# A mixture-of-experts stage on one core: the last expert's fourth up slot comes in as two transfers, and the combination stands ahead of every fourth up slot

## The reference

```python
# w_gu: (32, 1024, 2048), w_dn: (32, 1024, 1024)
def expert_block(args):
    xe, e = args
    gu = xe @ w_gu[e] + b_gu[e]
    x_glu = jnp.minimum(gu[:, :D_FF], SWIGLU_LIMIT)
    x_lin = jnp.clip(gu[:, D_FF:], -SWIGLU_LIMIT, SWIGLU_LIMIT)
    act = (x_lin + 1) * (x_glu * jax.nn.sigmoid(SWIGLU_ALPHA * x_glu))
    return act @ w_dn[e] + b_dn[e]

yb = lax.map(expert_block, (xb, block_e))
y = jnp.zeros((T + 1, D), h.dtype).at[slot_tok].add(yb.reshape(n_slots, D) * slot_w[:, None])
```

## Time and profile before

| what | value |
|---|---|
| median of 3 runs | 1636.06 us (1634.86 to 1638.85) |
| the profiled execution | 1637.52 us |
| its span in the trace | 1635.7 us |
| PE busy | 1600.7 us, 98% of the span |
| DVE busy | 685.6 us, 42% |
| ACT busy | 280.7 us, 17% |
| weights of the experts | 192 transfers of 2048 KB |

### The profile page before, as it was taken

How to read it: one execution, slowest core, us unless ns; L and a number is a source line. 1 busy time by engine, 2 the same in 40 slices (tenths; PEclk the granted TensorE clock), 3 DMA queues, 4 the chain that set the end, 5 groups by cost and what they waited for, 6 DMA issues and landing times.

```text
span 1635.7 us, 21977 instructions
## 1 busy us (share of the span) xinstructions
PE 1600.7 (98%) x8501; PEld 833.9 (51%) x8502; DVE 685.6 (42%) x1321; ACT 280.7 (17%) x590; POOL 8.1 (0%) x5
## 2 busy tenths in 40 slices
PE   6999999999999999999999999999989999999998
PEld 3787885333333333333333333333236598699953
DVE  2977743312121212221212121212145886688883
ACT  3215522101010000000000010100032242122311
POOL 0010000000000000000000000000000000000000
PEclk9999999999999999999999999999999999999999
DMA  9794637899999999999999999999993252454410
GB/s 398 295 386 181 258 116 264 331 408 427 428 429 428 428 429 428 429 429 428 429 428 428 430 428 428 429 428 428 427 428 117 91 220 103 165 195 155 173 73 26
DMA packets 38827, 529.47 MB, mean 324 GB/s; under 512 B 4352, under 2 KB 4752, under 8 KB 6512
## 3 DMA queue, kind: packets, MB, share of 16 engines
q1 hardware_dynamic: 36720, 521.16, 76.5%
q10 hardware_dynamic: 2048, 7.49, 1.2%
HBM read 527.58 MB, written 1.06 MB: 323 GB/s over the span
## 4 chain that ended last, share of the span: by engine, by line
PE 70%; DMA 28%; DVE 1%; ACT 0%; issue 0%; SPq 0%; DVEq 0%; ACTq 0%
DMA arena_ring<-experts_dram 27%; PE scores L2865 14%; PE att_out L2894 8%; PE proj L3262 5%; PE proj L2702 3%; PE proj L3159 3%; PE proj L2987 3%; PE proj L2518 3%; PE proj L2449 3%; PE scores L3317 2%; PE scores L3262 2%; PE proj L2822 2%; PE proj L2619 2%; PE proj L2481 2%; PE proj L2439 2%; PE turned L2811 2%
## 5 line engine op out<-in xcount | busy, mean ns | idle before, releaser
L2865 PE MATMUL scores<-arena_ring 128*64 128x512 f32 x2112 | 468.1, 594 | 9.3 <-DMA arena_ring<-experts_dram 8.8
L2865 PEld LDWEIGHTS scores<-arena_ring 128*64 128x64 f32 x2112 | 150.6, 137 | 314.7 <-issue 292.6
L2894 PE MATMUL att_out<-arena_ring 128*64 128x512 f32 x1056 | 241.1, 598 | 0.0
L1848 DVE COPY arena_ring<-turned 128x512 f32<-128x512 f32 x33 | 22.8, 692 | 345.4 <-PE turned L2811 345.4
L2894 PEld LDWEIGHTS att_out<-arena_ring 128*64 128x64 f32 x1056 | 69.9, 136 | 145.4 <-issue 118.3
L1058 ACT ACTIVATE arena_ring<-arena_ring 128x512 f32<-128x512 f32 x33 | 20.8, 630 | 476.3 <-DVE arena_ring L1851 476.3
L1755 DVE TENSOR_SCALAR arena_ring<-cst,arena_ring 128x128 f32<-128x128 f32 x68 | 20.5, 344 | 160.3 <-PE turned L2900 160.2
L1851 DVE TENSOR_SCALAR arena_ring<-scores 128x512 f32<-128x512 f32 x33 | 22.8, 692 | 152.5 <-PE scores L2865 152.5
L3262 PE MATMUL proj<-arena_ring 128*128 128x128 f32 x672 | 76.3, 275 | 0.0
L3262 PEld LDWEIGHTS proj<-arena_ring 128*128 128x128 f32 x672 | 75.6, 192 | 0.7 <-ACT arena_ring L1078 0.7
L2822 PE MATMUL proj<-arena_ring 64*128 64x512 f32 x264 | 65.6, 615 | 0.8 <-ACT arena_ring L1067 0.8
(11 more groups left out here) (504 smaller groups left out, 1791.5 us busy)
## 6 DMA issues: line engine op xcount, KB each, us to landing
arena_ring<-experts_dram SPq DMA_DIRECT2D x192, 2048.0 KB, 27.6
arena_ring<-stream_dram SPq DMA_DIRECT2D x53, 2048.0 KB, 10.1
arena_ring<-stream_dram SPq DMA_DIRECT2D x4, 1024.0 KB, 20.8
arena_ring<-bias_dram ACTq DMA_DIRECT2D x1, 2048.0 KB, 14.5
arena_ring<-gain_rows_dram ACTq DMA_DIRECT2D x3, 512.0 KB, 7.8
xtok<-xtok_dram SPq DMA_DIRECT2D x1, 1024.0 KB, 5.6
arena_ring<-ctxtok_dram SPq DMA_DIRECT2D x1, 1024.0 KB, 7.9
arena_ring<-mod_rows_dram ACTq DMA_DIRECT2D x2, 512.0 KB, 11.7
```

The costliest lines, as they stand in the source:

```text
L2865: ins = mm(AS[n][parts, :], xe[:, k % 4, k // 4, :], weights(s, kk * 2 * D + n * D + feats.start), start=False, stop=k == KD - 1, skip_gro ...
L2894: ins = mm(AO[parts, :], act_s[:, kk, s - 4, :], weights(s, kk * D + feats.start), start=s == 4 and kk == 0, stop=s == 5 and kk == 3)
```

## The change

The change has three parts. (1) The last expert's fourth up slot is issued as two transfers of 1 MB. The first brings the gate columns and signals a semaphore of its own, the second the linear columns; PE waits for each ahead of the columns that it uses. For this the host lays out each up slot with all gate columns first, and PE's column index is changed to match. (2) For every item but the first, `combine(0)` and `combine(1)`, with the wait on `yb_c`, stand ahead of the fourth up slot; before, they stood behind `turn(AO, xg)`. (3) Two semaphores at the program's start become one.

```diff
@@ sync
                     sp.wait_ge(landed[s], last)
+                    if place == NE - 1 and s == 3:
+                        for at, signal in ((0, gate_half_in), (SLOT // 2, landed[s])):
+                            sp.dma_start(wheel(place_of(place, s))[:, at:at + SLOT // 2],
+                                         part_of(bass.ds(e, 1), s)[:, at:at + SLOT // 2]).then_inc(signal, 16)
+                        continue
                     sp.dma_start(wheel(place_of(place, s)), part_of(bass.ds(e, 1), s)).then_inc(landed[s], 16)
@@ scalar
-            nc.scalar.activation(cse, cc, ACT.Tanh, scale=0.5).then_inc(cs_exp, 1)
+            nc.scalar.activation(cse, cc, ACT.Tanh, scale=0.5).then_inc(cs_steps, 1)
@@ vector
-            dve.wait_ge(cs_exp, 1)
+            dve.wait_ge(cs_steps, 1)
             step(V.tensor_scalar(cse, cse, 0.5, 0.5, ALU.mult, ALU.add))
-            V.tensor_tensor(cs[:, :, 0:2], cc, cse, ALU.mult).then_inc(cs_ready, 1)
+            V.tensor_tensor(cs[:, :, 0:2], cc, cse, ALU.mult).then_inc(cs_steps, 1)
@@ tensor
-            pe.wait_ge(cs_ready, 1)
+            pe.wait_ge(cs_steps, 2)
...
-                    weights_landed(s)
+                    if s == 3 and not first:
+                        pe.wait_ge(yb_c, i)
+                        combine(0)
+                        combine(1)
+                    split = place == NE - 1 and s == 3
+                    if split:
+                        pe.wait_ge(gate_half_in, turn_ * 16 - (NE - 2) * 16)
+                    else:
+                        weights_landed(s)
                     columns = [(kk, n) for kk in range(2) for n in range(2)]
                     if s == 3:
                         columns = [(kk, n) for n in range(2) for kk in range(2)]
                     for kk, n in columns:
                         k = 2 * s + kk
+                        if split and (kk, n) == (0, 1):
+                            weights_landed(s)
                         for parts, feats in halves:
                             ins = mm(AS[n][parts, :], xe[:, k % 4, k // 4, :],
-                                     weights(s, kk * 2 * D + n * D + feats.start),
+                                     weights(s, n * 2 * D + kk * D + feats.start),
...
                 pe.wait_ge(xg_ready, i + 2)
-                if not first:
-                    pe.wait_ge(yb_c, i)
                 turn(AO, xg).then_inc(xg_t, 1)
-                if not first:
-                    combine(0)
-                    combine(1)
                 pe.wait_ge(ohb_ready, i + 2)
                 pe.wait_ge(actv_ready, i + 1)
                 turn(PT, act_t).then_inc(act_turned, 1)
@@ host
-    gu = get("w_gu")[0].reshape(NE, 4, 2, P, 2 * D).transpose(0, 1, 3, 2, 4).reshape(NE, 4, P, SLOT)
+    gu = get("w_gu")[0].reshape(NE, 4, 2, P, 2, D).transpose(0, 1, 3, 4, 2, 5).reshape(NE, 4, P, SLOT)
```

More of the change, by code:

```diff
@@ L396, in two_blocks @@
         dve_evac = sem("dve_evac")
-        cs_ready = sem("cs_ready")
+        cs_steps = sem("tanh_then_spread_of_c_made")
         mod_slots = sem("mod_slots_used")
-        cs_exp = sem("cs_exp")
+        gate_half_in = sem("gate_columns_of_last_up_slot_landed")
         sq_ready = sem("squares_ready")
```

## The result

The changed kernel took 1683.37 us (median of 6, 1681.09 to 1685.74), the kernel before 1635.87 (median of 6). The ratio is 1.0282, 95% interval 1.0265 to 1.0300: slower by 47.5 us. The forecast was 1675.5, 39.4 us slower, in a range of 1666 to 1687.

The account below looks back on a forecast made before the run. PE was taken to bound the expert stage once 12.4 us of spare time were used; items growing from 27.10 to 28.72 us put its last item's first down block 39.4 us later: 1636.06 + 39.4 = 1675.5 us, range 1666 to 1687.

Parts of the forecast that it names:

- What bounds the kernel: Expert stage: PE needs 27.10 us an item, transfers 29.36 us an expert, but PE starts far behind; balanced on an edge.
- The slack of 12.4 us: Expert stage: all that PE has to spare before added work delays the last item's first down block; 0.39 us an item.
- The item: Each of 32 items: the moved combination costs 1.92 us, less 0.30 regained; 28.72 us, between 28.49 and 28.89.
- The chain gives back: Behind the fourth up slot: without the combination there, the second turn starts 0.30 us sooner, bounds 0.24 to 0.35.
- The total: Whole kernel: +39.4 us, bounds +32.1 to +44.9, set on the median: 1675.5 us; chance 0.80.
- the clock rival: New gaps of about 1.6 us between turns: the clock falls; +49 us if in every item, about 1724 us; chance 0.10.
- The mild case of that rival: Clock falls in the new gap in one of four items: 12 us more, about 1688 us.
- What the profile would show: Items about 28.7 us, DVE waits totalling near 50 us, no weight waits, full clock, last down block near 1242 us.
- The move is half hidden: Rival, each item: moved matmuls run partly beside neighbouring slots; item 27.5 to 28.4 us, 0 to +29 us; chance 0.05.
- Part 1 worth nothing in the changed kernel: Last expert's fourth up slot: the split saves nothing if PE is late, since both halves have landed long before.
- The transfers bind and PE's work is free: Rival, expert stage: the move costs under 0.39 us an item; -4.2 us, about 1632 us; chance 0.05.
- The row that was to decide: Up product: 512-column records start 0.218 us apart, against 0.213 at one column a cycle; no room for 1.92 us more.

Follow-up runs that it names:

- every_fifth: Changed kernel, but the combination moved only in every fifth turn and the last, old place otherwise: 1639.13 us, ratio 1.0011 to the kernel before.
- two_of_five: Changed kernel, but the combination moved only in two of five turns and the last, old place otherwise: 1650.03 us, ratio 1.0078 to the kernel before.
- move_only: Changed kernel without the split of the last expert's fourth up slot, combination still moved in every item but the first: 1683.92 us, ratio 1.0284.
- last_only: Changed kernel with the split, but the combination moved only in the last expert's turn: 1636.6 us, ratio 0.9997 to the kernel before.
- gains_last_only: Kernel before, only ScalarE's two loads of gain rows in the last item issued later, behind the copy of SelWT: 1647.6 us, ratio 1.0072.

## Why the prediction was right, point by point

**What bounds the kernel: right.** The slack of 12.4 us in the stage was the number on which all hung, and every_fifth and two_of_five measured it from both sides. The changed kernel shows the same from the other end: SP waits for PE, the weights land in 14.2 us at the median instead of 27.6, and the transfers nearly stand still from 800 to 820 us. (15.5 x 2.26 is 35 us and not the 34 of the prediction; nothing was worked out from it.)

**The item: the mechanism right, its size 0.17 us too small.** 28.72 was forecast, 28.89 measured; the forecast's upper bound was 28.89. Two terms were off. The switch between the combination's 128-column weights and the up slots' 64-column ones was taken at nothing within a bound of 0.11; the slots around it take 3.53 + 3.58 us to the next start instead of 6.97, 0.14 more. So the bound was set too low for this term. The chain gives back 373.78 - 371.52 = 2.26 us in place of 2.50, which is 0.24; I took 0.30 as the mean of the middle item's reading (0.24) and the first item's (0.35). The middle item's was the right one for the 32 items like it. 32 x 0.17 = 5.4 us, and 39.4 + 5.4 = 44.8 us is the stage's 43.3 + 1.6 us, where 1.6 is the earlier start of the second item in this execution.

**The total: in the range by its margin.** The stage's 44.9 us are the forecast's high bound, since one term fell on the dear end of its bound and the other beyond it. With the stretch behind the stage and the medians' part the measured 1683.37 us lies 1.0 above the highest value that was worked out for the forecast, 1682.4. It is in the range of 1666 to 1687 only by what was added for the clock rival, which did not happen in the items; that part of being right is luck. The mild case of that rival, 1688, was not in the range as the prediction says, but 1 us above it.

**What the profile would show: right in the stage.** The wait of 1.6 us in 33 items, 52.6 us in total, no wait for weights, and the same combination are there. The stage's last down block was put near 1242 and starts at 1245.97; the 1242.02 above is its first, which was put at 1238.2. And what is behind the stage took 1.7 us more, not the same time.

**"The move is half hidden": it was not.** The combination takes 366.02 to 367.94, the same 1.92 us, in its new place.

**Part 1 worth nothing in the changed kernel: right.** The two halves land 9.3 and 11.3 us after their issue at 1195.5 and 1196.0, and PE uses them from 1234.60. move_only, without the split, is as slow as both together.

**The clock rival: did not happen in the items.** With 32 more gaps of 1.6 us the granted clock stayed at 1.00 from 290 to 1255 us. The price given for one slow stretch, 1.53 us, was about right (1.7 behind the stage), and such stretches came elsewhere, in both kernels: the changed kernel's six executions have spans of 1679.3 us at a mean clock of 1.000 to 1683.9 at 0.997. So 1.7 us of the traces' difference come from where these stretches fall. That the same holds for the 2.5 us by which the medians differ more than the traces is likely and not shown.

**"The transfers bind and PE's work is free": wrong as given, in its size too.** The rule of the Trainium skill (Perfetto Trace Analysis, Identifying the Most-Contended Engine), as the prediction took it, pointed to the transfers, by the fuller resource and by the weight loads' share; the page names the share of peak work beside that one, which I did not work out. The trace disagrees: with the transfers' share at 1.01 and weight loads busy for 9.20 of 27.09 us, 1.79 us more of PE an item cost 43 us in the stage. The rival's price of -4.2 us was wrong by the same slip as the expectation of last_only. From the third slot's start at 1183.49 us, that slot, the combination, the fourth slot and the chain in a row end at 1183.49 + 3.53 + 1.92 + 3.58 + 2.26 = 1194.8 and not at 1192.9.

**The row that was to decide: a right answer by a weaker reason than it seemed.** The prediction set the spacing of 0.218 us against 512 columns at one a cycle, 0.213. But behind the stage of the kernel before, records of 512 columns with 128-column weights start 0.438 us apart (12 in 1220.95 - 1215.69 = 5.26 us) at a granted clock of 1.00. One column a cycle does not give that spacing, so nearness to 0.213 alone is no proof that PE is full. What proves it is the change itself: 1.92 us of matmuls ahead of the slot took 1.92 us.

## What to carry to other kernels

A piece of work that stands between a result and the wait for what is made from it is free up to the length of that wait (here 1.68 of 1.92 us: the chain's 2.26 less the first turn's 0.58); moved to where its engine is busy it costs all of itself, and the gap that it leaves stays. When an engine and the transfers run side by side with a deep buffer, compare whole stages (this engine's sum against the stage), not the rates of one item: here PE was faster than the transfers in each item and still bound the stage once 12.4 us were used up. When one of several waits is taken away, work out again what the next change would fill, since here the split had nearly emptied the wait that the move was to use.

## What the runs showed of the hardware

- Two loads of 512 KB on ScalarE's queue, issued at 1173.1 and 1173.5 us, delayed a 2 MB transfer that SP had issued at 1157.7 us: it took 31.7 us to land, and 29.4 in gains_last_only, where they come later. The delay of 2.3 us is about what their 1 MB takes at 428 GB/s, 2.4 us. The Trainium skill states that transfers started by different engines run on the same DMA engines and interleave (DMA: Bandwidth & Descriptors, Issuing engines are not separate DMA queues). This trace agrees, by those 2.3 us. The two loads took 11.6 and 17.4 us themselves; in the changed kernel, where they are issued behind a stretch in which SP's transfers move 27 GB/s, they took 3.4 and 4.9 us.
- A pause of 1.6 us on PE between two short turns, in 32 items of the changed kernel, never came with a lower clock. One of 2.48 us in the same place had a granted clock of 0.55 behind it, one of 2.38 us ahead of an up slot 0.51, and one of 1.79 us behind the stage was followed by the lower level in some executions and not in others.
- Nor did every lower clock follow a pause: in last_only PE works without a gap from 315.98 to 336 us and beyond, and the granted clock is 1.00 from 317 to 328 us and 0.51 from 328 to 332.
- Records of 512 columns start 0.218 us apart with 64-column weights and 0.438 with 128-column weights, both at a granted clock of 1.00. Going from one kind to the other and back cost 0.14 us an item (3.53 + 3.58 us against 6.97).
- A wheel of ten slots took the transfers from full rate to 63 GB/s for 20 us and back, and PE had no wait for weights.
